# Seven products instead of eight in the last two projections of a hybrid decoder layer

## The reference

```python
xn = rmsnorm(x, norm_w)
proj = xn @ w_in                       # 1024 -> 10248 columns: q k v i f o z b c x z_c g_m g_c
h = mlstm(q, k, v, i, f)               # 4 heads, matrix memory
h = rmsnorm_per_head(h) * head_norm_w * sigmoid(o) * silu(z_m)
y_m = h @ w_proj_m                     # 1024 x 1024
cv = short_conv(c_g * x_c, conv_w)     # width 3
y_c = (silu(z_c) * b_g * cv) @ w_proj_c
mix = sigmoid(g_m) * y_m + sigmoid(g_c) * y_c
out = x + mix @ w_out
y = rmsnorm(out, final_norm_w)
```

## Time and profile before

| | us |
|---|---|
| median of 3 runs | 2363.55 (2358.3 to 2364.69) |
| span of the profiled execution, first to last instruction | 2356.7 |
| matrix engine busy | 2323.1 (99%) |
| vector engine busy | 1488.1 (63%) |
| scalar engine busy | 948.6 (40%) |
| GpSimd busy | 77.5 (3%) |
| phase_c, from its first projection matmul to that of phase_d | 1786.4 to 2158.4 |
| phase_d to its last matmul | 2158.4 to 2349.6 |

### The profile page before, as it was taken

The page is one execution under the profiler, slowest core; times in us unless marked ns, Lnnn a source line. Parts: engine busy times, 40 slices in busy tenths (PEclk is TensorE's granted clock), DMA queues, the critical chain, the costliest instruction groups (busy, mean ns, idle before and its releaser), DMA issues. The chain is left out here.

```text
span 2356.7 us, 41040 instructions
## 1 busy us (share of the span) xinstructions
PE 2323.1 (99%) x14643; PEld 2254.8 (96%) x14643; DVE 1488.1 (63%) x2703; ACT 948.6 (40%) x1717; POOL 77.5 (3%) x84
## 2 busy tenths in 40 slices
PE   8999999999999999999999999999999999999998
PEld 8998999999999999999999999999998999998886
DVE  4447788898876687777776677777755333324333
ACT  3224444444454444455655444555554101002121
POOL 0011000000110000000020000000000000000000
PEclk9999999999999999999999999999999999999999
DMA  6665655455775765656765766557567433443442
GB/s 224 209 215 136 199 187 181 157 177 176 232 220 174 232 202 184 191 159 195 240 191 177 235 202 195 188 175 217 176 185 260 156 102 110 138 143 126 138 138 86
DMA packets 424977, 425.66 MB, mean 181 GB/s; under 512 B 32810, under 2 KB 363690, under 8 KB 424870
## 3 DMA queue, kind: packets, MB, share of 16 engines
q1 hardware_dynamic: 424870, 424.25, 56.9%
HBM read 297.36 MB, written 126.85 MB: 180 GB/s over the span
## 5 line engine op out<-in xcount | busy, mean ns | idle before, releaser
L1658 PE MATMUL b_g<-x_hi,w_hi 128*128 128x344 f32 (+1 forms) x3024 | 985.5, 326 | 9.0 <-DVE rows L1333 4.3
L1658 PE MATMUL b_g<-x_lo,w_hi 128*128 128x344 f32 (+1 forms) x3024 | 967.9, 320 | 0.0
L1658 PE MATMUL b_g<-x_hi,w_lo 128*128 128x344 f32 (+1 forms) x3024 | 967.0, 320 | 0.0
L1658 PEld LDWEIGHTS b_g<-x_hi,w_hi 128*128 128x128 f32 x3024 | 569.3, 188 | 16.1 <-DVE rows L1333 4.4
L1658 PEld LDWEIGHTS b_g<-x_lo,w_hi 128*128 128x128 f32 x3024 | 569.3, 188 | 1.7
L1658 PEld LDWEIGHTS b_g<-x_hi,w_lo 128*128 128x128 f32 x3024 | 569.4, 188 | 0.0
L1155 ACT ACTIVATE w_hi<-w_operands 128x512 fp32r<-128x512 f32 x519 | 323.5, 628 | 272.9 <-PE b_g L1658 261.2
L1295 DVE TENSOR_TENSOR w_lo<-w_operands,w_hi 128x512 fp32r<-128x512 f32 x519 | 354.2, 695 | 1.2
L1155 ACT ACTIVATE w_hi<-stages 128x512 fp32r<-128x512 f32 x216 | 134.7, 629 | 138.3 <-PE b_g L1658 119.4
L1295 DVE TENSOR_TENSOR w_lo<-stages,w_hi 128x512 fp32r<-128x512 f32 x216 | 145.6, 684 | 7.7 <-ACT w_hi L1155 6.9
L2017 PE MATMUL c_g<-act_hi,RH 128*128 128x294 f32 x448 | 134.4, 300 | 2.1 <-DVE rows L1948 2.1
(11 more groups left out here) (305 smaller groups left out, 3116.0 us busy)
## 6 DMA issues: line engine op xcount, KB each, us to landing
w_operands<-w_in SPq DMA_DIRECT2D x282, 256.0 KB, 5.2
stages<-w_ops_d SPq DMA_DIRECT2D x36, 768.0 KB, 5.5
w_operands<-w_ops_d SPq DMA_DIRECT2D x34, 768.0 KB, 4.9
stages<-w_in SPq DMA_DIRECT2D x72, 256.0 KB, 3.8
w_operands<-w_ops_d SPq DMA_DIRECT2D x70, 256.0 KB, 6.3
w_ops_d<-w_operands SPq DMA_DIRECT2D x18, 768.0 KB, 3.3
w_ops_d<-stages SPq DMA_DIRECT2D x18, 768.0 KB, 3.4
w_ops_d<-w_operands SPq DMA_DIRECT2D x36, 256.0 KB, 3.9
```

The source lines that it names most:

```text
L1658: last = nc.tensor.matmul(bank[:, 0:n], w[:, j, k, :], x[:, k, 0:n], start=(j < 4 and k == 0 and m == 0), stop=(k == 3 and m == 2), skip_g ...
```

## The change

The two branch projections and the output projection use the seven-product scheme of `phase_b`, with its block operands.

- Tokens are cut into 4 groups of 2 x 258 columns, and the outer loop is over the branch, then the group, then 4 pairs of output blocks: 32 "pairs" (`NPAIR`) of seven products each, the whole written out without loops. The gate loads wait for the gate before (`gated`), and so do stores and accumulations. A branch's split weights (`WH`, `WL`, 4 blocks of 7 operands) stay in SBUF for its 4 groups; the blocks of the next branch, and then of the output projection, replace them one by one while the last group's pairs run (`AHEAD`, `RAW_AT`).
- Activations are loaded per group as quarters; GpSimd forms four sums (`act_sum`), the high and low splits of the seven operands follow (`act_high`, `act_low`) into one set of buffers, during the last pair of the group before.
- Weight sums are made by VectorE, for blocks 8 to 11 by GpSimd (`POOL_SUMS`).
- Per pair, ScalarE copies two results out of PSUM, VectorE makes five adds of 258 columns, and then one gate instruction over 1032 elements. The first branch's gated rows are stored to `mix_d`, the second's are added to them in DRAM by DMAs that GpSimd issues with `accum_op=add`.
- The head norm's weight is applied to the z rows by ScalarE in `phase_b` (24 more instructions over 688 or 680 elements). The first block's raw weights and the first quarters are loaded, and partly summed, at the end of `phase_b`.
- The output projection takes 8 pairs of 128-token tiles with seven products of 4 x 3 matmuls of 512 columns; the 8 sample tokens have a plain product of 48 matmuls.

```diff
-TN = 294
-NTC = 7
+TN = 258
+NG = 4
+TP = 2 * TN * NG
+NPAIR = 4 * NG * 2
...
+COARSE = [(2, 4), (0, 2), (4, 6), (6, 7)]
+FINE = [(0, 1), (4, 5), (1, 2), (5, 6), (2, 3), (3, 4), (6, 7)]
...
+def weight_sum(eng, engine, g, b, at):
+    r, e = raw_buffer(g, b), sum_buffer(g)
+    if at == 0:
+        engine.wait_ge(*raw_signal(g, b))
+        if b:
+            engine.wait_ge(g.w_ready, pieces_before(b))
+        eng.tensor_tensor(e[:, 1], r[:, 1], r[:, 3], ALU.add).then_inc(g.w_sum, 1)
...
+def act_sum(nc, pool, g, s, at):
...
+    elif at == 2:
+        pool.wait_ge(g.x_ready, 7 * s + 1)
+        pool.wait_ge(g.xq_sum, 4 * s + 2)
+        nc.gpsimd.tensor_tensor(a, c, d, ALU.subtract).then_inc(g.xq_sum, 1)
...
@@ phase_b, ScalarE @@
-                        nc.scalar.activation(ZT[:, 0:n], ER[:, q, 1, 0:n], ACT.Tanh, scale=0.5).then_inc(z_set, 1)
+                        nc.scalar.activation(ZT[:, 0:n], ER[:, q, 1, 0:n], ACT.Tanh, scale=0.5)
+                        nc.scalar.activation(ER[:, q, 1, 0:n], ER[:, q, 1, 0:n], ACT.Copy,
+                                             scale=g.hnw[:, bass.ds(2 * i + q, 1)]).then_inc(z_set, 1)
...
@@ phase_c @@
+    AHEAD = {0: 1, 1: 2, 2: 3, 13: 4, 14: 5, 16: 6, 17: 7, 29: 8, 30: 9, 31: 10}
+    RAW_AT = {0: 1, 1: 2, 2: 3, 4: 4, 14: 5, 15: 6, 17: 7, 18: 8, 28: 9, 30: 10, 31: 11}
+    POOL_SUMS = {28: 8, 30: 9, 31: 10}
...
@@ phase_c, SyncE @@
+            for n in range(NPAIR):
+                s = n // 4 + 1
+                if n:
+                    load_tanh(n)
+                    if n <= NPAIR // 2:
+                        store(n - 1)
...
+                if n % 4 == 0:
+                    sp.wait_ge(g.x_ready, 7 * s)
...
+                    load_acts(sp, g, s)
+                if n in RAW_AT and n:
+                    raw_weights(RAW_AT[n])
...
@@ phase_c, GpSimd @@
+            for n in range(NPAIR):
...
+                if n > NPAIR // 2:
+                    accumulate(n - 1)
+                if n % 4 == 2:
+                    act_sum(nc, pool, g, n // 4 + 1, 0)
+                    act_sum(nc, pool, g, n // 4 + 1, 1)
+                if n in POOL_SUMS:
+                    for at in range(4):
+                        weight_sum(nc.gpsimd, pool, g, POOL_SUMS[n], at)
+                if n % 4 == 3:
+                    act_sum(nc, pool, g, n // 4 + 1, 2)
+                    act_sum(nc, pool, g, n // 4 + 1, 3)
...
@@ phase_c, VectorE @@
+            for j in range(NOP):
+                split_low(nc, dve, g, 0, j)
+                act_low(nc, dve, g, 0, j)
+            for n in range(NPAIR):
+                for j in range(NOP):
+                    if j == 0:
+                        if n - 1 in AHEAD:
+                            ahead(AHEAD[n - 1], 7)
+                        if n and n % 4 == 0:
+                            act_low(nc, dve, g, n // 4, NOP - 1)
+                        if n:
+                            gate(n - 1)
+                    step(n, j)
+                    if n in AHEAD:
+                        ahead(AHEAD[n], j)
+                    if n % 4 == 3 and j:
+                        act_low(nc, dve, g, n // 4 + 1, j - 1)
...
@@ phase_c, TensorE @@
+            for n in range(NPAIR):
+                br, t, p = place(n)
+                for j in range(NOP):
+                    if t == 0:
+                        pe.wait_ge(g.w_ready, pieces_for(4 * br + p, j))
+                    if p == 0:
+                        pe.wait_ge(g.x_ready, 7 * (n // 4) + j + 1)
...
+                    elif j == 4:
+                        pe.wait_ge(copied, 2 * n + 1)
+                    elif j == 5:
+                        pe.wait_ge(ev, 5 * n + 2)
+                    elif j == 6:
+                        pe.wait_ge(ev, 5 * n + 3)
```

More of the change, by code:

```diff
@@ L165, in phase_a, with act_low @@
+def act_low(nc, dve, g, s, j):
+    high, low = act_parts(g, s, j)
+    dve.wait_ge(g.x_hi, 7 * s + j + 1)
+    nc.vector.tensor_tensor(low, act_source(g, s, j), high.bitcast(F32), ALU.subtract).then_inc(g.x_ready, 1)
 def phase_a(nc, g):
@@ L1602, in body @@
                             x_low(p + 1, j - 1)
+                        if extra == "end" and q == 1 and 2 <= j < 6:
+                            weight_sum(nc.vector, dve, g, 0, j - 2)
                     if extra == "turn" and q == 1:
@@ new lines, in _, with accumulate @@
+        @block.gpsimd
+        def _(pool):
+            act_sum(nc, pool, g, 0, 2)
+            act_sum(nc, pool, g, 0, 3)
+            def accumulate(n):
+                pool.wait_ge(gated, n + 1)
+                pool.dma_start(two_rows(g.mix_d, n), MX[n % 2], accum_op=ALU.add).then_inc(g.acc_out[n % 2], 16)
+            for n in range(NPAIR):
+                if n == NPAIR // 2:
+                    for par in range(2):
+                        pool.wait_ge(mix_out[par], 16 * NPAIR // 4)
+                if n > NPAIR // 2:
[9 more added lines that the diff above has]
+                    act_sum(nc, pool, g, n // 4 + 1, 3)
+            accumulate(NPAIR - 1)
@@ L2012, in _ @@
+            gate(NPAIR - 1)
+            ahead(AHEAD[NPAIR - 1], 7)
+            act_low(nc, dve, g, 2 * NG, NOP - 1)
         @block.tensor
         def _(pe):
[L2014 to L2020 removed]
@@ L2129, in _ @@
+            for par in range(2):
+                sp.wait_ge(y_out[par], 16 * (NT2 // 2 + 1 - par))
         @block.gpsimd
@@ L2165, in _ @@
+            for i in range(NT2):
+                if i + 1 < NT2:
+                    for at in range(4):
+                        act_sum(nc, pool, g, S0 + i + 1, at)
+                if i:
+                    rstd(i - 1)
+            rstd(NT2 - 1)
+            rstd(NT2)
         @block.scalar
         def _(act):
-            def square(i, par):
-                n = rows(i)
-                act.wait_ge(summed, i + 1)
-                nc.scalar.activation(junk[:n, :], Y[par][:n, :], ACT.Square, accum_out=stat[:n, 0, par:par + 1]).then_inc(squared, 1)
@@ L2172, in _, with square @@
-            with_lookahead(act, hi, square)
+            for j in range(NOP):
+                act.wait_ge(g.c_done, 7 * NPAIR)
+                split_high(nc, act, g, LASTW, j)
+            def square(i, a):
+                rows = P if i < NT2 else NS
+                act.wait_ge(summed, 2 * i + a + 1)
+                if i or a:
+                    act.wait_ge(squared, 2 * i + a)
+                nc.scalar.activation(junk[:rows, :], Y[i % 2][:rows, a], ACT.Square, accum_out=stat[:rows, 0, a:a + 1]).then_inc(squared, 1)
@@ new lines, in _ @@
+            i = NT2 - 1
+            residual(i, 0)
+            residual(i, 1)
+            variance(i)
+            normed(i, 0)
+            normed(i, 1)
+            dve.wait_ge(done, 7 * NT2 + 1)
+            dve.wait_ge(x_in[0], 16 * (NT2 // 2 + 1))
+            dve.wait_ge(y_out[0], 16 * (NT2 // 2))
+            for h in range(2):
+                last = nc.vector.scalar_tensor_tensor(out=Y[0][:NS, 0, h * N:(h + 1) * N], in0=G[h][:NS, :], scalar=0.5,
+                                                      in1=X[0][:NS, 0, h * N:(h + 1) * N], op0=ALU.mult, op1=ALU.add)
@@ new lines, in _ @@
+            pe.wait_ge(sx_set, 3)
+            pe.wait_ge(copied, 2 * (NT2 - 1))
+            pe.wait_ge(ev, 5 * (NT2 - 2) + 1)
+            for h, operands in enumerate((((0, 0), (1, 4)), ((0, 3), (2, 5)))):
+                step = 0
+                for a, j in operands:
+                    for k in range(4):
+                        for x, w in ((SH, g.WH), (SH, g.WL), (SL, g.WH)):
+                            last = nc.tensor.matmul(G[h][:NS, :], x[:, a, k, :], weights(w, j, k),
+                                                    start=(step == 0), stop=(step == 23))
+                            step += 1
@@ L2219, in phase_d @@
+            last.then_inc(done, 1)
     ctx.close()
```

770 lines of the change are left out of this document (407 added, 363 removed).

## The result

Median 2413.56 us of four runs (2410.4 to 2417.11) against 2361.03 for the kernel before (2358.3 to 2364.69): ratio 1.0223, 95% interval 1.0208 to 1.0239. The direction was the one forecast; the size was not: +52 us instead of +13, outside the range. The profiled execution has a span of 2408.7 us against the 2356.7 of the earlier trace rows.

A forecast was written before the change was run, and what follows sets the result against it. The matrix engine, busy 99% of 2356.7 us, was taken as the bound. Savings of -67.9 and added waits and clock gave +14.8, taken as +13: span 2369.7, with 6.9 carried 2376 us; range 2328 to 2402.

The forecast's parts named there:

- Matmuls: Narrower matmuls at 120.5 ns in the projection stage, -41.9 us; 96 fewer matmuls in the output stage, -22.3 us.
- Turns: Pairs with seven activation splits, some held by GpSimd sums, delay product 5 of the next pair; six turns, +13 us.
- First pair: Projection stage start: low splits queue before the first add and raw weights land late; pair 1 starts 13.9 us later.
- Pairs 1, 2 and 13 to 17: Product 6 waits on late raw weights and sums: 15.1 us in pairs 1 and 2, 19.6 in pairs 13 to 17.
- Border: Projection to output stage: the matrix engine waits for late splits, gate and adds; 13 us instead of 1.9, +11.1.
- Output stage, "hidden or small": Output stage: 12 us of vector work hides under 19.5 us of matmuls per tile pair; first output pair +1.
- Clock: About ten gaps of 2 us and more lower the granted clock, 1.6 us each; half counted, +8 us.
- the 2 that I had taken off: Projection stage's first pair: its loads meet an empty queue, so 2 us were taken off the sum of +14.8.
- rival (4): Weight loads set the matmul pace, 136 ns stay: +42, 2418 us; chance 0.04.
- Rivals (2): Waits are short, the vector engine rarely held and weights landing early: waits of 37, 2333 us; chance 0.27.
- (3): In between: some 60 us of waits, 2356 us, from 2350 to 2366; chance 0.13.
- "under 7": Projection stage: an accumulating DMA's 516 KB lands in under 7 us, within some 14 allowed; cost 0.

The follow-up runs named there:

- run 1: Changed kernel with SyncE issuing the output stage's activation loads for each tile pair one iteration earlier; 2391.75 us against 2413.56.
- run 4: Changed kernel with GpSimd's four activation sums of groups 1 to 7 touching one element each, so operands are not the right ones; 2392.13 us against 2413.56.
- run 8: Changed kernel with two of the four activation sums of a turn moved from GpSimd to VectorE; 2402.25 us against 2413.56.
- Run 2: Changed kernel with SyncE issuing raw weights of blocks 2, 3, 5, 6, 7 before the gate load and store; 2385.94 us against 2413.56.
- Run 7: Changed kernel with VectorE's weight sums placed behind the add after product 3 instead of before it; 2412.95 us against 2413.56.
- run 3: Changed kernel with only the last accumulating DMA (pair 31) moved into the output stage, behind GpSimd's four weight sums; 2409.61 us against 2413.56.
- run 9: Changed kernel with plain SyncE stores in place of GpSimd's 16 accumulating DMAs, the merge of the branches left out; 2407.34 us against 2413.56.
- Run 5: Changed kernel with the weight sums of blocks 9 and 10 (pairs 30 and 31) moved from GpSimd to VectorE; 2409.81 us against 2413.56.
- run 6: Changed kernel with block 7 summed and split one pair later, in pair 18 instead of 17; 2410.1 us against 2413.56.
- the first combination: Changed kernel with the edits of run 1, Run 2, run 3, Run 5, run 6 and run 8 together; 2351.57 us, ratio 0.996 to the kernel before.

## Why the prediction was right in direction and wrong in size

**Matmuls, -41.9 and -22.3: right.** 119.9 ns a matmul against 120.5 forecast (1.6 us more saved). The output stage shows -21.2 as soon as its waits are gone (run 1).

**Turns, +13: 12.5, right in mechanism and size.** What the earlier trace rows shows holds; runs 4 and 8 take it away and two pairs with a turn get 2.0 and 1.5 us shorter. The Trainium skill's rule ("SBUF — State Buffer", section "SBUF: two separate sides") holds here too: a split of 1.23 us takes 3.38. Splits beside GpSimd do not keep their 1.2 us.

**First pair, +13.9: 14.5.** The timeline follows the forecast to 0.6 us (last split 17.8 us into the stage, 18.4 forecast; pair 1 starts at 27.6, 27.0 forecast).

**Pairs 1, 2 and 13 to 17, +34.7: 46.3.** The mechanism was right; the mis-sized term was "with that gate over at T+3.2, landing is T+3.2+7.9". It is gate + 11.4. I priced four issues at the earlier trace rows and a load at the earlier trace rows, both from queues with nothing beside them. Here a gate load and a store go first: the issues take 3.4 us and the weights land 6.7 us after their issue. Run 2, the same load in front, gets 3.7 us and gives back 27.6 us. Run 7 shows that moving the sums within VectorE's order gives nothing back.

**Border, 13: 20.4.** 5.4 us of it is the stage's end waiting for GpSimd's DMA to land. I had carried the 0.9 us of the earlier trace rows over, from a stage that ended with no such DMA (runs 3 and 9). The step that failed is "then 0.9 for the border itself". From VectorE's last instruction to the first matmul it is 7.8 us where 2.2 were forecast, and 2.3 in runs 3 and 9. VectorE itself is through 12.6 us behind the matrix engine, 10.5 forecast. Pair 31 (+5.9) comes on top. I had counted the matrix engine through it in 10.5 us and put GpSimd's chain for block 9, in the pair before, at nothing. Run 5 takes 2.0 us of it away, and in run 9, without the accumulation in front of that chain, the pair takes 10.3 us.

**Output stage, "hidden or small", +1: 20.5.** This is the step that failed in kind, not in size. I put 12 us of vector work under 19.5 us of matmuls and called the sum hidden. The work fits; its data don't come in time. I never followed SyncE's list: the loads for the next pair of tiles stand behind the store of the last one, so the work for the next pair begins 12.6 us into a pair, and 3.4 us into it in run 1. Run 1 moves one line and the 12 us are hidden.

**Clock, +8: about 31 us of slow matmuls.** In the projection stage 101.7 us are extra, of which 78.2 are waits (58.7 in the rows above, less 1.0 before the first product, and 20.4): 23.5 us are slow matmuls. In the output stage run 1 shows 7.5. I had counted ten gaps of 2 us and more and taken half of 1.6 us for each. The number was near, the size was not. The trace has ten stretches of slow matmuls: two in pair 0, one each from pairs 1, 2, 14 and 17, and four in the output stage, with 1.7 to 4.2 us of slow matmuls each. Not every wait brings one, as I had expected: the six waits of the turns (1.6 to 1.7 us) do not, and the clock reads 1.00 from 1872 to 1884, behind the first of them. How much of the 23.5 us a full clock would give back is not shown. Where the landing bounds a pair, a slow matmul only shortens the wait behind it, so these are parts of the matrix engine's time and not prices.

The sum: waits of the projection stage and border 3.6 more than forecast, the clock there 15.5, the output stage 19.5 (its share of the clock included), the pace -1.6, the start 1 and the 2 that I had taken off: 40, against the 39 between 2369.7 and 2408.7. That the time got longer, as forecast, owes as much to these misses as to the terms that were right: slower had a chance of 0.50, and the forecast was +13.

**Rivals.** The weight loads don't set the pace (119.9 ns); that the time lies near the 2418 of rival (4) is a coincidence. Rivals (2) and (3) wanted fewer waits than there are. The accumulation is slower than "under 7" but not too slow: the 16 land in 6.2 to 10.1 us, 8.4 in the median, under the 14 allowed; VectorE waits for rows to be stored or added only twice, 3.4 us in all. The Trainium skill's fit ("DMA: Bandwidth & Descriptors", "Anatomy of one DMA — SWDGE (gpsimd) path") gave 3.2 us as an estimate; the measured ones take two to three times that, beside other traffic. What the accumulation costs is its place in GpSimd's list: 7.7 us of the gap at the border and 5.7 us in the pair before it (run 9), of which 6.0 come back as a loss in pair 28.

**Left open.** Single gains of 1, 2, 3, 5, 6 and 8 add up to 71.9 us and the first combination gave 62. Its pairs 18 and 19 explain about half (34.9 us together, 29.5 in run 6); the rest was not traced. How much of the 10.5 us at the border could go without a stage's end there wasn't tried.

## What to carry to other kernels

Before calling work hidden, follow the queue that brings its data: ask not only whether an engine's work fits under the matmuls but when its first input lands, and what the issuing queue waits for in front of it. A transfer's price depends on what stands ahead of it; put the one with a deadline first, and don't issue it behind stores that nobody waits for. And a wait that is removed in one place can land beside a GpSimd instruction in another: after each shift, look at what the two engines do in the same microseconds.

## What the hardware showed that was not expected

- A stage that ends with an accumulating DMA of GpSimd's in flight waits until it has landed (5.8 us from the last vector instruction to the next stage, 6.2 us from issue to landing); with that DMA moved it is 0.3 us, and a store of SyncE's in flight (3.7 us to landing) holds nothing.
- After a wait of 3.3 us the granted clock read 0.70 and 0.73 over the next 6 us; after one of 2.1 us it read 1.00 for 9 us, and after others of 2.1 us it fell to 0.56 to 0.59 for 3 us. In the output stage 11.8 us of waits cost 19.3.
- Issues of SyncE are not of fixed cost: four loads of 256 KB took 2.0 us on an idle queue, 3.4 behind two others and 4.7 to 6.8 behind four loads of activations.
- GpSimd's own sums are slowed as well: 512 elements took 1.3 us alone and 1.6 to 2.3 beside VectorE's splits.
